# Split halves placed at multiples of 1024 bytes, and held activations stored with high and low half of each element side by side

## The chip, the core and the metric

The kernel runs as one program on one NeuronCore of a Trainium2 chip. Its five engines (TensorE, VectorE, ScalarE, GpSimd and SyncE, in the rows PE, DVE, ACT, POOL and SP) each work through their own list of instructions and meet at semaphores; weights come from HBM through DMA queues into SBUF, the on-chip memory of 128 partitions. PEld in the rows is TensorE's weight load, the reading of the operand that the array holds while the other operand streams through it. The metric is the device time of one execution in microseconds.

## What is computed

Three transformer-like blocks follow each other on one sequence of 256 tokens with 1024 features. Cut to the matrix products that matter here:

```
for layer in range(2):                      # first block
    h = rms_norm(x, g_mix[layer])
    qkv = h @ w_in[layer]                   # 1024 x 3072
    mix = attention of three kinds (differential, block-causal, dilated)
    x = x + mix @ w_out[layer]              # 1024 x 1024
    h2 = rms_norm(x, g_ffn[layer])
    u = causal_conv3(h2 @ w_up[layer])      # 1024 x 5632
    x = x + (silu(gate) * val) @ w_down[layer]   # 2816 x 1024
# second block: a state-space branch and a sparse attention branch, then
h = h + merged @ w_out_2
# expert layer: every token picks 128 of 16384 experts
q = hn @ peer_wq; scores; top-k; gates
act = gelu(hn . u_tab[expert]) * gate       # computed densely: hn @ u_tab.T, 16384 columns
h = h + act @ v_tab                         # 16384 x 1024
return rms_norm(h)
```

Everything is float32, and the result must be close to float32.

## The kernel before

**How a product is made exact.** TensorE reads operands here in the type `float32r`, a shortened float32. To keep the precision, each operand is split into a high half (rounded by the write into an F32R tile) and a low half (the original minus the high half, again rounded). A product is then three matmuls into the same PSUM bank: high with high, high with low, low with high. `mm3` (L536 to L543) writes them out for each step k of the contraction, and nearly all the work of the kernel goes through its line L542. In its calls the first argument pair is held in the array (128 columns), the second is streamed.

**How the weights get in.** The weights are cut into `plan` units of 128 x 1024 floats (512 KB). SyncE loads one unit after the other into the tiles `raw0` to `raw5` (L512), ScalarE writes its high half into `wh` (L1112), and VectorE (L1461) or GpSimd (L2117) writes the low half into `wl`; the list `lower` says which of the two, fixed by the unit's number. Buffers are reused in turn: six of each up to the stage `keys`, four of each in the two last stages.

**Two ways round.** In one kind of stage the weights are held and the activations stream (256 columns for a matmul): the up projection (`wup`, 44 units in each layer), the query projection of the expert layer (`wpq`, 16 units) and the first expert product (`ut`, 128 units). One unit is 8 steps x 3 matmuls = 24 matmuls of 256 columns. In the other kind the activations are held and the weights stream (512 columns): `win` and `wout` (24 and 8 units in each layer), `wdown` (22 in each layer), `wout2` (8) and the second expert product (`vt`, 128). One unit is 12 matmuls of 512 columns. Both ways stream 6144 columns for a unit. A few stages of the second block use whole float32 operands, unsplit (`hw` with `raw`).

**The tiles of activations.** `hh` and `hl` hold high and low half of the normalised and transposed activations, 8 steps of 256 tokens, and serve both kinds of stage; `yh` and `yl` hold those of the gated activations before `wdown`; `ach0/ach1` and `acl0/acl1` those of the expert activations, one unit each. ScalarE writes the high halves (L1142 in `turned`, L1179 in `out_turned`, others inside the stages), VectorE writes the low halves of h (L1511 in `halves_low`) and of the expert activations, GpSimd writes `yl` (L2122). All are written with an element step of one, and the matmuls read them with an element step of one.

**Where the tiles lie.** SBUF is handed out in the order of the `scoped` calls, after 16384 bytes of DMA scratch and a few constants. Start of a tile within 1024 bytes, before and after the change, as the built programs have it:

| tile | before | after |
|---|---|---|
| raw0..3, wh0..3, wl0..3 | 608 | 0 |
| raw4..5, wh4..5, wl4..5 | 0 | 0 |
| hh, hl (after: h2) | 640 | 0 |
| yh, yl (after: y2) | 0 | 0 |
| ach, acl (after: ac0, ac1) | 608 | 0 |

**The order of the work.** It is written out by hand: each engine has one function (`sp`, `pe`, `act`, `dve`, `pool`) that lists its instructions with their waits. Within `ut`, TensorE does `hidden(j)` for unit j, and from `J_GATE` = 59 on also the gate products of four tokens after each unit (`gates_of`). For the units before 59 GpSimd makes the low halves, after that VectorE. In `vt`, each unit waits for its `acl` (L1069) and its low half.

## Time and profile before

| | |
|---|---|
| time, median of 3 runs | 1750.53 us (1750.17 to 1751.01) |
| profiled execution, its span | 1747.2 us |
| PE busy | 1691.7 us (97%), 10714 matmuls |
| PEld busy | 1454.8 us (83%) |
| DVE, ACT, POOL busy | 1149.2, 821.6, 706.5 us |
| HBM read | 279.33 MB, 161 GB/s over the span |

A busy TensorE is not yet a TensorE at its peak: what counts is the **pitch**, the time from the start of one matmul to the start of the next. It can be read from a timeline, or as busy time over count in a stretch without gaps.

### The profile page before, as it was taken

Reading aid. Unit: us, or ns where it says so; the run is one execution under the profiler, and the core shown is the slowest. Engines: PE = TensorE matmul, PEld = TensorE weight load, DVE = VectorE, ACT = ScalarE, POOL = GpSimd, SP = SyncE. Lnnn points to the kernel's source line nnn. Section 1 sums busy time; section 2 is a strip of 40 time slices with the busy share of each in tenths; the row PEclk is TensorE's granted clock in tenths of the full one; section 3 lists DMA queues with packets and bytes.
Section 4 is the critical chain, followed back from the end, with each engine's and each line's share of the span. In section 5 each row is a group of like instructions: output and inputs, shape, how many; then the busy total and the mean of one; then the engine's idle time right before and its main releaser. Section 6 shows DMA issues by size and latency. Waiting matters only on the chain.

```text
span 1747.2 us, 27224 instructions
## 1 busy us (share of the span) xinstructions
PE 1691.7 (97%) x10714; PEld 1454.8 (83%) x10714; DVE 1149.2 (66%) x2422; ACT 821.6 (47%) x1453; POOL 706.5 (40%) x384
## 2 busy tenths in 40 slices
PE   7999999999999998999999999999999999999997
PEld 6779998777799986544579999999999988888885
DVE  6655785756367576666332999999999644444443
ACT  5455665354476642113243554544444455555553
POOL 2424667132357721432163999700000144444443
PEclk9999999999999999999999999999999999999998
DMA  7333545463255564323353656544444566666664
GB/s 292 112 109 132 182 162 195 150 217 108 74 193 190 173 203 134 111 87 109 95 194 134 216 167 198 179 147 145 145 140 139 160 193 193 194 194 195 195 193 134
DMA packets 77455, 283.20 MB, mean 162 GB/s; under 512 B 8720, under 2 KB 8976, under 8 KB 77072
## 3 DMA queue, kind: packets, MB, share of 16 engines
q1 hardware_dynamic: 76032, 276.50, 48.8%
q10 hardware_dynamic: 1296, 4.97, 0.8%
q8 instruction: 85, 1.39, 0.3%
q14 instruction: 42, 0.34, 0.1%
HBM read 279.33 MB, written 2.10 MB: 161 GB/s over the span
## 4 chain that ended last, share of the span: by engine, by line
PE 78%; DVE 8%; ACT 5%; POOL 5%; issue 3%; DMA 1%; POOLq 0%; DVEq 0%; ACTq 0%
PE bank L542 62%; PE bank L533 7%; PE bank L597 5%; POOL wl L2117 4%; ACT wh L1112 2%; DVE att L1478 2%; PE bank L665 1%; DVE wl L1461 1%; ACT att L1115 1%; PE bank L967 1%; PE bank L889 1%; DVE ssb L1467 1%; DVE mix L1506 1%; DVE xs L1467 1%; PE bank L837 0%
## 5 line engine op out<-in xcount | busy, mean ns | idle before, releaser
L2117 POOL TENSOR_TENSOR wl<-raw,wh 128x1024 fp32r<-128x1024 f32 x213 | 548.0, 2584 | 699.6 <-ACT wh L1112 691.1
L542 PE MATMUL bank<-hh,wh 128*128 128x256 f32 x1856 | 526.2, 284 | 5.5 <-POOL wl L2117 4.8
L1112 ACT ACTIVATE wh<-raw 128x1024 fp32r<-128x1024 f32 x476 | 492.7, 1050 | 57.2 <-PE bank L542 40.8
L542 PE MATMUL bank<-hl,wh 128*128 128x256 f32 x1856 | 519.1, 280 | 0.0
L542 PE MATMUL bank<-hh,wl 128*128 128x256 f32 x1856 | 518.1, 279 | 0.0
L1461 DVE TENSOR_TENSOR wl<-raw,wh 128x1024 fp32r<-128x1024 f32 x263 | 352.8, 1347 | 98.7 <-ACT wh L1112 98.2
L542 PEld LDWEIGHTS bank<-hh,wh 128*128 128x128 f32 x1856 | 349.1, 188 | 7.0 <-POOL wl L2117 6.0
L542 PEld LDWEIGHTS bank<-hl,wh 128*128 128x128 f32 x1856 | 349.2, 188 | 0.0
L542 PEld LDWEIGHTS bank<-hh,wl 128*128 128x128 f32 x1856 | 349.0, 188 | 0.0
L1467 DVE TENSOR_TENSOR acl<-H,ach 128x256 fp32r<-128x256 f32 x128 | 87.5, 685 | 181.6 <-ACT ach L1115 181.6
L542 PE MATMUL bank<-wh,ach 128*128 128x512 f32 x512 | 199.3, 389 | 0.4 <-DVE acl L1467 0.4
L542 PE MATMUL bank<-wh,acl 128*128 128x512 f32 x512 | 199.2, 389 | 0.0
L542 PE MATMUL bank<-wl,ach 128*128 128x512 f32 x512 | 199.2, 389 | 0.0
L1115 ACT ACTIVATE H<-bank 128x256 f32<-128x256 f32 (+32 forms) x199 | 64.7, 325 | 240.6 <-PE bank L542 208.0
L1115 ACT ACTIVATE ach<-H 128x256 fp32r<-128x256 f32 x128 | 53.4, 418 | 172.7 <-PE bank L542 172.2
L542 PE MATMUL bank<-wh,hh 128*128 128x512 f32 x288 | 119.3, 414 | 5.5 <-DVE hl L1467 2.9
L1478 DVE SCALAR_TENSOR_TENSOR att<-bank,sml,att 128x255 f32<-128x255 f32 (+1 forms) x176 | 84.4, 480 | 56.7 <-ACT att L1115 53.5
L542 PE MATMUL bank<-wh,hl 128*128 128x512 f32 x288 | 114.1, 396 | 0.0
L542 PE MATMUL bank<-wl,hh 128*128 128x512 f32 x288 | 113.9, 396 | 0.0
L542 PEld LDWEIGHTS bank<-wh,ach 128*128 128x128 f32 x512 | 96.1, 188 | 20.7 <-issue 0.6
L542 PEld LDWEIGHTS bank<-wh,acl 128*128 128x128 f32 x512 | 96.1, 188 | 20.0
L542 PEld LDWEIGHTS bank<-wl,ach 128*128 128x128 f32 x512 | 96.1, 188 | 19.7
(216 smaller groups left out, 2313.4 us busy)
## 6 DMA issues: line engine op xcount, KB each, us to landing
raw<-in_ut_dram SPq DMA_DIRECT2D x128, 512.0 KB, 3.5
raw<-in_vt_dram SPq DMA_DIRECT2D x128, 512.0 KB, 3.8
raw<-in_wup_dram SPq DMA_DIRECT2D x88, 512.0 KB, 4.2
raw<-in_win_dram SPq DMA_DIRECT2D x48, 512.0 KB, 4.6
raw<-in_wdown_dram SPq DMA_DIRECT2D x44, 512.0 KB, 4.2
raw<-in_wout_dram SPq DMA_DIRECT2D x24, 512.0 KB, 3.6
raw<-in_wga_dram SPq DMA_DIRECT2D x16, 512.0 KB, 3.6
raw<-in_wpq_dram SPq DMA_DIRECT2D x16, 512.0 KB, 5.1
```

What stands on the lines that cost most here:

```text
L533: m = p.e.matmul(out, l, r, start=i == 0, stop=i == len(pairs) - 1)
L542: m = p.e.matmul(out, lhs[i][a], rhs[i][b], start=start and i == 0 and j == 0, stop=stop and i == n - 1 and j == 2)
L597: m = p.e.matmul(banks[b][:, 0:cw], whole[:, off + h * kper + k, tcols(t)], unit_whole(i, k, kper, slice(0, cw)), start=h == 0 and k == 0, ...
L665: m = p.e.transpose(banks[b][:, 256 * (i % 2) + 128 * k:256 * (i % 2) + 128 * k + 128], buf[:, o:o + 128], ids[:, :])
L889: s = p.e.matmul(banks[yb][o:o + 32, 0:256], l[:, 32 * n:32 * n + 32], turned_z[n % 2][:, a, b, :], start=j == 0, stop=j == 3, tile_positi ...
L967: m = p.e.matmul(banks[b][:, :], hTw[:, 2 * h + k, tcols(t)], unit_whole(i, k, 2, slice(0, 512)), start=h + k == 0, stop=h + k == 2)
L1112: a.e.activation(high_of(u), raw_of(u), ACTF.Copy).then_inc(act_hi.up(("hi", u)), 1)
L1115: a.e.activation(out, src, f, **kw).then_inc(act_out.up(ev), 1)
L1461: v.e.tensor_tensor(low_of(u), raw_of(u), high_of(u).bitcast(F32), ALU.subtract).then_inc(dve_lo.up(("lo", u)), 1)
L1467: v.e.tensor_tensor(out, a, b, op).then_inc(dve_out.up(ev), 1)
L1478: v.e.scalar_tensor_tensor(out, a, s, b, op0, op1).then_inc(dve_out.up(ev), 1)
L2117: g.e.tensor_tensor(low_of(u), raw_of(u), high_of(u).bitcast(F32), ALU.subtract).then_inc(pool_lo.up(("lo", u)), 1)
```

## The change

Three things are done together:

- Padding is added (a tile `pad0` of 96 floats, `sta` grown to 768, `con` to 1664, `sml` to 896, `R_AT` to 16896), and the DMA scratch is cut from 16384 to 1024 bytes to make room. With it every tile of a split operand starts at a multiple of 1024 bytes (table above).
- `hh`/`hl` become one tile `h2` of 4096 floats with two readings. Before a stage that streams the activations (`halves_for` gives `hT_moving`, norms named "f") it is laid out as before, high half first, then the low half. Before a stage that holds them (`hT_held`) the high half of element i is at 2i and its low half at 2i + 1.
- `yh`/`yl` and `ach`/`acl` become `y2` and `ac2`, always side by side.

So 2928 matmuls (864 with h, 528 with y, 1536 with the expert activations) hold an operand that is read with an element step of 2, and ScalarE, VectorE and GpSimd write, and in part read, these tiles with a step of 2. No instruction is added, removed or moved on any engine, and shapes and types are the same; all that differs besides is that one wait of ScalarE for VectorE inside `ut` falls one weight split later, since `R_AT` has moved.

```
--- before.py
+++ after.py
@@ -100,20 +100,21 @@
...
+        scoped(ctx, "pad0", 96)
         xs = scoped(ctx, "xs", 2048)
...
         sc_h = ExitStack()
-        hh, hl = scoped(sc_h, "hh", 2048, F32R), scoped(sc_h, "hl", 2048, F32R)
+        h2 = scoped(sc_h, "h2", 4096, F32R)
         sc_h.close()
         hw, sel_s = scoped(ctx, "hw", 2048), scoped(ctx, "sel_s", 2048)
-        sta = scoped(ctx, "sta", 760)
+        sta = scoped(ctx, "sta", 768)
         raws = [scoped(ctx, f"raw{i}", 1024) for i in range(4)]
...
         early = ExitStack()
-        con_s = scoped(early, "con", K_W - 128)
-        sml_s = scoped(early, "sml", S_W)
+        con_s = scoped(early, "con", 1664)
+        sml_s = scoped(early, "sml", 896)
         tab_s = scoped(early, "tab", 8192)
...
@@ -127,7 +128,8 @@
...
         sc_f = ExitStack()
-        yTh, yTl = [scoped(sc_f, f"y{c}", NTILE * 256, F32R)[:, :].rearrange("p (k t) -> p k t", k=NTILE) for c in "hl"]
+        y2 = scoped(sc_f, "y2", 2 * NTILE * 256, F32R)[:, :].rearrange("p (k t a) -> p a k t", k=NTILE, a=2)
+        yTh, yTl = y2[:, 0], y2[:, 1]
         sc_f.close()
...
@@ -146,8 +148,8 @@
...
         sc_oh.close()
-        ach = [scoped(ctx, f"ach{j}", 256, F32R)[:, :] for j in range(2)]
-        acl = [scoped(ctx, f"acl{j}", 256, F32R)[:, :] for j in range(2)]
+        ac2 = [scoped(ctx, f"ac{j}", 512, F32R)[:, :].rearrange("p (t a) -> p a t", a=2) for j in range(2)]
+        ach, acl = [a[:, 0] for a in ac2], [a[:, 1] for a in ac2]
         banks = [ctx.enter_context(nc.psum_tensor(f"bank{i}", [128, 512], F32)) for i in range(8)]
...
@@ -282,8 +284,8 @@
...
         x = xs[:, :].rearrange("p (t d) -> p t d", t=2)
-        hTh = hh[:, :].rearrange("p (k t) -> p k t", k=8)
-        hTl = hl[:, :].rearrange("p (k t) -> p k t", k=8)
+        hT_moving = h2[:, :].rearrange("p (a k t) -> p a k t", a=2, k=8)
+        hT_held = h2[:, :].rearrange("p (k t a) -> p a k t", k=8, a=2)
         hTw = hw[:, :].rearrange("p (k t) -> p k t", k=8)
...
@@ -302,8 +304,11 @@
...
-        def hT(k, cols):
-            return hTh[:, k, cols], hTl[:, k, cols]
+        def halves_for(st):
+            return hT_moving if st[0] == "f" else hT_held
+
+        def hT(k, cols, of=hT_held):
+            return of[:, 0, k, cols], of[:, 1, k, cols]
...
@@ -434,8 +439,8 @@
...
         H = H_s[:, :].rearrange("p (j t) -> p j t", j=128)
-        R_AT = 16800
-        assert R_AT >= K_W - 128 + S_W + 8192 + 6144
+        R_AT = 16896
+        assert R_AT >= 1664 + 896 + 8192 + 6144
         r_at = [R_AT]
...
@@ -614,7 +619,7 @@
...
                             m = mm3(banks[b][:, 0:256], [unit_pair(i, k, kt, tcols(c)) for k in range(kt)],
-                                    [hT(off + k, ALLC) for k in range(kt)], True, True, ready)
+                                    [hT(off + k, ALLC, hT_moving) for k in range(kt)], True, True, ready)
                         else:
...
@@ -796,7 +801,7 @@
...
                         m = mm3(banks[b][:, 256 * half:256 * half + 256], [unit_pair(i, k, 8, tcols(0)) for k in range(8)],
-                                [hT(k, ALLC) for k in range(8)], True, True, ready_both(("f", L)))
+                                [hT(k, ALLC, hT_moving) for k in range(8)], True, True, ready_both(("f", L)))
                         m.then_inc(pe_out.up(("used", i), ("up", L, f, half)), 1)
...
@@ -1038,7 +1043,7 @@
...
                 claim(b)
-                m = mm3(banks[b][:, 0:256], [unit_pair(i, k, 8, tcols(0)) for k in range(8)], [hT(k, ALLC) for k in range(8)], True, True, ready_both(("f", 2)))
+                m = mm3(banks[b][:, 0:256], [unit_pair(i, k, 8, tcols(0)) for k in range(8)], [hT(k, ALLC, hT_moving) for k in range(8)], True, True, ready_both(("f", 2)))
                 m.then_inc(pe_out.up(("used", i), ("hid", j)), 1)
...
@@ -1139,7 +1144,7 @@
...
                         a.wait_ge(pe_out, ("T", st, t, k))
-                        do(hTh[:, k:k + n, tcols(t)], quad(ps("T", st, t, k), n), ACTF.Copy, ("hTh", st, t, k))
+                        do(halves_for(st)[:, 0, k:k + n, tcols(t)], quad(ps("T", st, t, k), n), ACTF.Copy, ("hTh", st, t, k))
...
@@ -1161,7 +1166,7 @@
...
             stream_up_to(first["win", 0])
-            load(con_s[:, :], consts_d[:, 128:K_W], con_in, "con")
+            load(con_s[:, 0:K_W - 128], consts_d[:, 128:K_W], con_in, "con")
             load(sml(0, S_W), smalls_d, sml_in, "sml")
...
@@ -1176,7 +1181,7 @@
...
                     a.wait_ge(pe_out, ("mT", L, g))
-                    do(hTh[:, 2 * g:2 * g + 2, :], ps("mT", L, g)[:, :].rearrange("p (k t) -> p k t", k=2), ACTF.Copy, ("mTh", L, g))
+                    do(hT_held[:, 0, 2 * g:2 * g + 2, :], ps("mT", L, g)[:, :].rearrange("p (k t) -> p k t", k=2), ACTF.Copy, ("mTh", L, g))
...
@@ -1506,14 +1511,14 @@
...
-            def halves_low(k0, n, cols, src, hi, ev):
+            def halves_low(of, k0, n, cols, src, hi, ev):
                 v.wait_ge(act_out, hi)
-                tt(hTl[:, k0:k0 + n, cols], src, hTh[:, k0:k0 + n, cols].bitcast(F32), ALU.subtract, ev, alone=True)
+                tt(of[:, 1, k0:k0 + n, cols], src, of[:, 0, k0:k0 + n, cols].bitcast(F32), ALU.subtract, ev, alone=True)
...
                     for k, n in parts(st, q0, nq):
-                        halves_low(k, n, tcols(t), quad(ps("T", st, t, k), n), ("hTh", st, t, k), ("hT", st, t, k))
+                        halves_low(halves_for(st), k, n, tcols(t), quad(ps("T", st, t, k), n), ("hTh", st, t, k), ("hT", st, t, k))
...
@@ -1733,7 +1738,7 @@
...
                 def out_turned(g):
-                    halves_low(2 * g, 2, ALLC, ps("mT", L, g)[:, :].rearrange("p (k t) -> p k t", k=2), ("mTh", L, g), ("mT", L, g))
+                    halves_low(hT_held, 2 * g, 2, ALLC, ps("mT", L, g)[:, :].rearrange("p (k t) -> p k t", k=2), ("mTh", L, g), ("mT", L, g))
...
@@ -2383,7 +2388,7 @@
...
-    nc = _bacc.Bacc("TRN2", target_bir_lowering=False, num_devices=1)
+    nc = _bacc.Bacc("TRN2", target_bir_lowering=False, num_devices=1, dynamic_dma_scratch_size=1024)
     made = layout(inputs)
...
     for name in _ORDER:
```

## Rows read from the trace of the kernel before

**Rows 1.** The page: engines, slices of the span (tenths busy), shares of the chain.
```profile
PE 1691.7 (97%) x10714; PEld 1454.8 (83%) x10714; DVE 1149.2 (66%) x2422; ACT 821.6 (47%) x1453; POOL 706.5 (40%) x384
PEclk9999999999999999999999999999999999999998
PE 78%; DVE 8%; ACT 5%; POOL 5%; issue 3%; DMA 1%; POOLq 0%; DVEq 0%; ACTq 0%
```

**Rows 2.** Chain that ended last, in time: start us, length us, work xcount (512 columns held).
```profile
141.01 5.61 PE bank L542 x24
...
296.02 41.35 PE bank L542 x177
...
611.93 55.18 PE bank L542 x239
...
1386.56 343.02 PE bank L542 x1512
```

**Rows 3.** The same chain, where weights are held (256) or operands are unsplit.
```profile
709.58 6.87 PE bank L597 x16
...
909.01 45.50 PE bank L542 x384
954.51 7.16 PE bank L533 x64
...
1050.23 53.22 PE bank L542 x456
```

**Rows 4.** Timeline of PE, second down projection, round a change of weight buffer: start us, us.
```profile
616.10 0.39 PE L542 MATMUL bank<-wh,yh 128*128 128x512 f32 x1
616.32 0.39 PE L542 MATMUL bank<-wl,yh 128*128 128x512 f32 x1
616.55 0.39 PE L542 MATMUL bank<-wh,yl 128*128 128x512 f32 x1
...
617.46 0.40 PE L542 MATMUL bank<-wh,yh 128*128 128x512 f32 x1
...
619.80 0.39 PE L542 MATMUL bank<-wl,yh 128*128 128x512 f32 x1
```

**Rows 5.** Stretches of the up projections: us, PE (x), PEld, DVE, ACT, POOL, clock, DMA.
```profile
165.00:280.00 115.00, 115.00 (x976) 115.00 (x975) 86.22 (x140) 70.47 (x121) 80.00 (x54) 1.00 0.54 181
505.00:610.00 105.00, 105.00 (x892) 105.00 (x892) 71.95 (x98) 66.44 (x113) 76.91 (x52) 1.00 0.54 181
```

**Rows 6.** Chain in the first expert product, where GpSimd holds it.
```profile
1021.20 19.98 POOL wl L2117 x5
...
1106.51 18.39 POOL wl L2117 x5
```

**Rows 7.** Stretches: attention, `ut` up to unit 59, after it, `vt`; columns as in rows 5.
```profile
20.00:160.00 140.00, 135.89 (x772) 107.94 (x771) 85.02 (x225) 72.39 (x165) 45.31 (x36) 1.00 0.38 125
...
959.00:1128.00 169.00, 164.24 (x1397) 163.02 (x1397) 158.13 (x422) 86.43 (x124) 154.40 (x58) 1.00 0.57 184
1128.00:1386.00 258.00, 258.00 (x2234) 257.93 (x2231) 245.60 (x719) 118.08 (x272) 4.05 (x2) 1.00 0.46 150
...
1400.00:1720.00 320.00, 320.00 (x1413) 265.05 (x1413) 153.45 (x177) 161.45 (x236) 141.16 (x59) 1.00 0.62 193
```

**Rows 8.** Groups: line engine op xcount | busy us, mean ns | idle before, releaser.
```profile
L1467 DVE TENSOR_TENSOR acl<-H,ach 128x256 fp32r<-128x256 f32 x128 | 87.5, 685 | 181.6 <-ACT ach L1115 181.6
...
L1115 ACT ACTIVATE ach<-H 128x256 fp32r<-128x256 f32 x128 | 53.4, 418 | 172.7 <-PE bank L542 172.2 <-DVE H L1467 0.5
L2122 POOL TENSOR_TENSOR yl<-att,yh 128x256 fp32r<-128x256 f32 x44 | 48.6, 1104 | 6.6 <-POOL att L2122 0.5
```

**Rows 9.** Waits of PE: line, waited for, us in total, times, longest.
```profile
PE bank L542 <- POOL wl L2117: 8.5, 11, 1.3
PE bank L542 <- DVE hl L1467: 3.6, 6, 1.1
```

More of the change, by code:

```diff
@@ L101, in scoped @@
             return where.enter_context(nc.sbuf_tensor(name, [128, n], dt))
+        scoped(ctx, "pad0", 96)
         xs = scoped(ctx, "xs", 2048)
@@ L106, in program @@
         sc_h = ExitStack()
-        hh, hl = scoped(sc_h, "hh", 2048, F32R), scoped(sc_h, "hl", 2048, F32R)
+        h2 = scoped(sc_h, "h2", 4096, F32R)
         sc_h.close()
         hw, sel_s = scoped(ctx, "hw", 2048), scoped(ctx, "sel_s", 2048)
-        sta = scoped(ctx, "sta", 760)
+        sta = scoped(ctx, "sta", 768)
         raws = [scoped(ctx, f"raw{i}", 1024) for i in range(4)]
@@ L114, in program @@
         early = ExitStack()
-        con_s = scoped(early, "con", K_W - 128)
-        sml_s = scoped(early, "sml", S_W)
+        con_s = scoped(early, "con", 1664)
+        sml_s = scoped(early, "sml", 896)
         tab_s = scoped(early, "tab", 8192)
@@ L129, in program @@
         sc_f = ExitStack()
-        yTh, yTl = [scoped(sc_f, f"y{c}", NTILE * 256, F32R)[:, :].rearrange("p (k t) -> p k t", k=NTILE) for c in "hl"]
+        y2 = scoped(sc_f, "y2", 2 * NTILE * 256, F32R)[:, :].rearrange("p (k t a) -> p a k t", k=NTILE, a=2)
+        yTh, yTl = y2[:, 0], y2[:, 1]
         sc_f.close()
@@ L148, in program @@
         sc_oh.close()
-        ach = [scoped(ctx, f"ach{j}", 256, F32R)[:, :] for j in range(2)]
-        acl = [scoped(ctx, f"acl{j}", 256, F32R)[:, :] for j in range(2)]
+        ac2 = [scoped(ctx, f"ac{j}", 512, F32R)[:, :].rearrange("p (t a) -> p a t", a=2) for j in range(2)]
+        ach, acl = [a[:, 0] for a in ac2], [a[:, 1] for a in ac2]
         banks = [ctx.enter_context(nc.psum_tensor(f"bank{i}", [128, 512], F32)) for i in range(8)]
@@ L284, in program @@
         x = xs[:, :].rearrange("p (t d) -> p t d", t=2)
-        hTh = hh[:, :].rearrange("p (k t) -> p k t", k=8)
-        hTl = hl[:, :].rearrange("p (k t) -> p k t", k=8)
+        hT_moving = h2[:, :].rearrange("p (a k t) -> p a k t", a=2, k=8)
+        hT_held = h2[:, :].rearrange("p (k t a) -> p a k t", k=8, a=2)
         hTw = hw[:, :].rearrange("p (k t) -> p k t", k=8)
@@ L303, in sml, with halves_for, hT @@
             return sml_s[:, c:c + n]
-        def hT(k, cols):
-            return hTh[:, k, cols], hTl[:, k, cols]
+        def halves_for(st):
+            return hT_moving if st[0] == "f" else hT_held
+        def hT(k, cols, of=hT_held):
+            return of[:, 0, k, cols], of[:, 1, k, cols]
         iota = con(K_IOTA, 128)
@@ L436, in program @@
         H = H_s[:, :].rearrange("p (j t) -> p j t", j=128)
-        R_AT = 16800
-        assert R_AT >= K_W - 128 + S_W + 8192 + 6144
+        R_AT = 16896
+        assert R_AT >= 1664 + 896 + 8192 + 6144
         r_at = [R_AT]
@@ L616, in by_features @@
                             m = mm3(banks[b][:, 0:256], [unit_pair(i, k, kt, tcols(c)) for k in range(kt)],
-                                    [hT(off + k, ALLC) for k in range(kt)], True, True, ready)
+                                    [hT(off + k, ALLC, hT_moving) for k in range(kt)], True, True, ready)
                         else:
@@ L798, in pe @@
                         m = mm3(banks[b][:, 256 * half:256 * half + 256], [unit_pair(i, k, 8, tcols(0)) for k in range(8)],
-                                [hT(k, ALLC) for k in range(8)], True, True, ready_both(("f", L)))
+                                [hT(k, ALLC, hT_moving) for k in range(8)], True, True, ready_both(("f", L)))
                         m.then_inc(pe_out.up(("used", i), ("up", L, f, half)), 1)
@@ L1040, in hidden @@
                 claim(b)
-                m = mm3(banks[b][:, 0:256], [unit_pair(i, k, 8, tcols(0)) for k in range(8)], [hT(k, ALLC) for k in range(8)], True, True, ready_both(("f", 2)))
+                m = mm3(banks[b][:, 0:256], [unit_pair(i, k, 8, tcols(0)) for k in range(8)], [hT(k, ALLC, hT_moving) for k in range(8)], True, True, ready_both(("f", 2)))
                 m.then_inc(pe_out.up(("used", i), ("hid", j)), 1)
@@ L1141, in turned @@
                         a.wait_ge(pe_out, ("T", st, t, k))
-                        do(hTh[:, k:k + n, tcols(t)], quad(ps("T", st, t, k), n), ACTF.Copy, ("hTh", st, t, k))
+                        do(halves_for(st)[:, 0, k:k + n, tcols(t)], quad(ps("T", st, t, k), n), ACTF.Copy, ("hTh", st, t, k))
             def exps(tag, maps, buf, i):
@@ L1163, in act @@
             stream_up_to(first["win", 0])
-            load(con_s[:, :], consts_d[:, 128:K_W], con_in, "con")
+            load(con_s[:, 0:K_W - 128], consts_d[:, 128:K_W], con_in, "con")
             load(sml(0, S_W), smalls_d, sml_in, "sml")
@@ L1507, in scale, with halves_low @@
                                              ).then_inc(dve_out.up(("nrm", st, t, q), ("used", row) if t and q else None), 1)
-            def halves_low(k0, n, cols, src, hi, ev):
+            def halves_low(of, k0, n, cols, src, hi, ev):
                 v.wait_ge(act_out, hi)
-                tt(hTl[:, k0:k0 + n, cols], src, hTh[:, k0:k0 + n, cols].bitcast(F32), ALU.subtract, ev, alone=True)
+                tt(of[:, 1, k0:k0 + n, cols], src, of[:, 0, k0:k0 + n, cols].bitcast(F32), ALU.subtract, ev, alone=True)
             def turned(st, ts_, nq, q0=0):
@@ L2384 @@
     from concourse.bass_utils import run_bass_kernel_spmd as _run
-    nc = _bacc.Bacc("TRN2", target_bir_lowering=False, num_devices=1)
+    nc = _bacc.Bacc("TRN2", target_bir_lowering=False, num_devices=1, dynamic_dma_scratch_size=1024)
     made = layout(inputs)
```

6 lines of the change are left out of this document (3 added, 3 removed).

## The prediction

> **What bounds the kernel now.** I read the page first: PE is busy 97% of the span, at full granted clock in every slice but the last, and 78% of the chain that ended last is PE's [rows 1]. PE waits for other engines only a few microseconds in all [rows 9]. So time can come only out of PE's pitch, the time from one matmul's start to the next, and I read that next, from the chain in order of time.
>
> With held activations and 512 streamed columns the pitch is 343.02/1512 = 226.9 ns in the second expert product, 5.61/24 = 233.8 ns with h, and (41.35 + 55.18)/(177 + 239) = 232.0 ns with y [rows 2]. With held weights and 256 streamed columns it is 53.22/456 = 116.7 ns in the first expert product, 45.50/384 = 118.5 in the query projection [rows 3] and (115 + 105)/(976 + 892) = 117.8 in the up projections [rows 5].
>
> What would it be without any loss? Unsplit float32 passes of 512 columns take 6.87/16 = 429.4 ns, and stream each column at half the pace; half of that, 214.7 ns, is my floor for 512 split columns [rows 3]. Weight loads set a floor of their own: where 128 columns are loaded for short streams the pitch is 7.16/64 = 111.9 ns [rows 3]. So each matmul of 512 loses 12 to 19 ns, and each of 256 some 5 to 7.
>
> **Where the loss depends on addresses.** The telling rows are those of the second `wdown` [rows 4]. Nothing changes there except the weight buffer: the stage begins in the buffers 4 and 5, which start at a multiple of 1024 like y itself, and goes on in 0 to 3, which start 608 bytes off. Before the switch two steps take 616.55 - 616.10 = 0.45 us, 226 ns each or so; after it, from 617.46 to 619.80, ten take 2.34, 234 ns each. The table of tile starts fits it in the other stages: the expert activations start like the weight buffers (both 608) and run at 226.9; h (640) never starts like any weight buffer and runs at 233.8. So equal starts within 1024 bytes are worth 6 to 7 ns of 233. I take the step to be proportional to the columns: a unit has 6144 of them either way, and takes 24 x 116.7 = 2.80 us with 256, and 12 x 233.8 = 2.81 us with 512 at unequal starts.
>
> **The change part by part.** *Alignment, 256 columns.* In all 5568 matmuls the two operands start unlike now (640 against 608 or 0). Half of the aligned 226.9 is 113.4 ns, above the load's floor of 111.9. Gain: 3072 x 3.3 + 384 x 5.1 + 2112 x 4.4 = 10.1 + 2.0 + 9.3 = 21.4 us. Bounds: no gain; a gain down to 111.9, which is 29.7; or, if an aligned matmul loses 12.2 ns however short it is (226.9 - 214.7), 107.4 + 12.2 = 119.6, a loss of about 13. I take the first, since the loss went with the columns above.
>
> *Alignment, 512 columns.* h goes from 233.8 to 226.9 (864 x 6.9 = 6.0 us), y from 232.0 (528 x 5.1 = 2.7), and the expert activations are aligned already. Together 8.7.
>
> *Element step of 2 in what is held.* No row shows a held operand with a step of 2, so it is bounded. The streamed operand moves on by 4 bytes per column. The load takes about twice as long per column (111.9 ns for 128 against 214.7 for 512), so with a step of one it advances at half the stream's pace or less, and the stream overtakes it; with a step of 2 both advance alike, and may get into a fixed relation. The unsplit float32 rows, in which both read at one slow pace, show no loss, but these have slack too. The good end is 214.7 ns. For the bad end: the load touches twice as many bytes' worth of memory, and if the loss comes from that, 12.2 becomes 24.4, 239.1 ns. I take the middle of the good end and the aligned row, (214.7 + 226.9)/2 = 220.8 ns, because equal pace is what differs from the losing rows, and the float32 rows are the nearest ones with equal pace. From 226.9 on that is 2928 x 6.1 = 17.9 us (5.3 with h, 3.2 with y, 9.4 with the experts).
>
> The Trainium skill ("SBUF — State Buffer", specifications) says that an SBUF line is 16 bytes and that two hits in a line suffice for full bandwidth, which a float32 step of 2 just has. No run here shows it; by it the step costs nothing.
>
> *Writes with a step of 2.* ScalarE's write of `ach` (418 ns) and VectorE's of `acl` (685) have 173 and 182 us of idle time ahead of them, over 128 units: even doubled they stay hidden [rows 8]. GpSimd's `yl` (1104 ns, 44 of them) has 80.00 busy of 115 us around it [rows 5]; doubled it would add at most 22 x 1.1 = 24 us to a layer's 35 to 45 of slack. Only h is written on the path, at the start of a stage: PE waits 3.6 us for `hl` [rows 9]. Unchanged it costs 0, doubled 3.6; I take 2.
>
> *What does not get through.* In the attention stages PE is busy 135.89 of 140 us [rows 7], but other engines stand in the chain between its matmuls; of the 11.3 us for h, 768/864 lie there, and I drop 3. Before unit 59, GpSimd holds the chain twice for five low halves (19.98 and 18.39 us, [rows 6]); a faster PE waits longer there, about ten units each at 24 x 3.3 = 79 ns, so I drop 1.6. After unit 59 VectorE is busy 245.60 of 258 us [rows 7]: 12.4 idle for 69 units, or 180 ns each against 79 needed. It covers, thinly; I drop 1. In `vt` ACT, DVE and POOL are busy about half the time and DMA 0.62; a unit at 12 x 220.8 = 2.65 us instead of 2.72 strains none.
>
> **Sum.** 21.4 + 8.7 + 17.9 = 48.0; less 2 + 3 + 1.6 + 1 = 7.6: 40 us. The profiled span of 1747.2 becomes 1707; it lies 3.3 under the median, so the time is 1750.5 - 40 = 1710.5, rounded to 1711.
>
> **The rivals.**
>
> *Alignment only.* The step of 2 does nothing, and 512 columns stay at 226.9 as in the expert stage: 48.0 - 17.9 = 30.1, less some 6.5, is 24: 1727. For it: the aligned expert rows are so steady over 1512 matmuls that they may be the natural pitch.
>
> *Clean.* Equal pace and equal start remove all loss: 214.7 for 512 adds 2928 x 6.1 = 17.9 more, less 2 not passed on: 1695, and 1687 if 256 comes down to 111.9 too. Against it: nothing split runs so today.
>
> *The step of 2 collides (slower).* Its place is PE's weight load beside the stream, in the 128 units of `vt` above all. With 239.1 ns: 1536 x 12.2 = 18.7, 864 x 5.3 = 4.6 and 528 x 7.1 = 3.7, together 27 lost against 21.4 won, plus 2 for the writes: 1758; and 1780 if 256 gains nothing. It decides from a 512 pitch of about 236 (today's mean is 229.9, and 21.4 less 2.6 of deductions over 2928 is 6.4).
>
> *Nothing.* The Trainium skill ("TensorE: Matmul & The Clock Gate", what happens when you issue a matmul) says that TensorE has two independent read ports, and that loading the next weights takes nothing from the running matmul. By that rule, starts and steps of what is held are without effect, and the time stays 1750.5. As a mechanism here: what looks like an effect of the starts [rows 4] would be one of the stage. The trace speaks against it, since pitch switches from 226 to 234 inside one stage.
>
> **How the numbers follow.** Forecast 0.40, alignment only 0.25, clean 0.15, collision 0.13, nothing 0.07. A difference of 0.2% (3.5 us) is what a measurement can tell from no change: faster 0.40 + 0.25 + 0.15 = 0.80, same 0.07, slower 0.13. The range goes from the clean case, where its 256 gains in part (1690), to the no-change case (1752), and leaves out the collision and the extreme of clean, under 0.2.
>
> **What would show it.** In the profile after, per matmul: `vt` at 220.8 instead of 226.9, h and y at the same value as `vt`, `ut` at 113.4, a unit of either kind near 2.65 to 2.72 us, and wup at 113.4 as well. If `vt` stays at 226.9 the step of 2 is idle; at 233 or more it collides. If `ut` stays at 116.7 or moves towards 119.6, the proportion to columns is wrong, and that term of 21.4, the largest, falls. The prediction also fails if the gain appears in PE's pitch but DVE after unit 59 or POOL before it becomes the chain: then PE's idle time there would rise from near zero.

## The result

The changed kernel is slower: 1770.97 us (median of 4 runs, 1770.85 to 1772.19) against 1750.57 us, a ratio of 1.0121 with a 95% interval of 1.0107 to 1.0134, or 20.4 us. The forecast was 1711, with a range of 1690 to 1752; the time lies outside it, and on the other side. The profiled span went from 1747.2 to 1769.2 us.

The page of the changed kernel shows PE busy for the same share of the span as before, at full granted clock: it works longer, and its share of the chain rose from 78% to 87% [rows 1].

```profile
PE 1717.6 (97%) x10714; PEld 1486.3 (84%) x10714; DVE 1144.0 (65%) x2422; ACT 824.0 (47%) x1453; POOL 709.0 (40%) x384
PE 87%; DVE 4%; POOL 4%; ACT 3%; issue 1%; DMA 1%; POOLq 0%; DVEq 0%; ACTq 0%
```

The chain of the changed kernel in order of time (start us, length us, work), the pieces that answer to [rows 2, 3]:

```profile
141.31 5.62 PE bank L547 x24
...
912.78 46.31 PE bank L547 x384
...
1056.14 54.73 PE bank L547 x456
...
1398.65 353.05 PE bank L547 x1512
```

The pitch of the second expert product is now 353.05/1512 = 233.5 ns (226.9 before), that of the first 54.73/456 = 120.0 (116.7), of the query projection 46.31/384 = 120.6 (118.5); with h held it is 5.62/24 = 234.2 (233.8). The up projections, from their stretches (us, PE (x), PEld, DVE, ACT, POOL, clock, DMA), stand at 220/1839 = 119.6 against 117.8 [rows 5]:

```profile
165.00:280.00 115.00, 115.00 (x961) 115.00 (x960) 86.39 (x140) 70.51 (x120) 79.83 (x54) 1.00 0.54 181
505.00:610.00 105.00, 105.00 (x878) 105.00 (x877) 70.47 (x94) 66.94 (x111) 75.86 (x52) 1.00 0.54 178
```

So 1536 x 6.6 = 10.1 us come from the second expert product, 3072 x 3.3 + 384 x 2.1 = 10.9 from the first and its query projection, 2112 x 1.8 = 3.8 from the up projections: 24.8 of pitch. The span grew by 22.0. PE's waits for GpSimd fell from 8.5 to 6.3 us [rows 9], which is most of the difference of 2.8: where another engine held PE before, a slower PE costs nothing.

```profile
PE bank L547 <- POOL wl L2122: 6.3, 9, 1.2
```

The writes with a step of 2 cost next to nothing, as the groups answering to [rows 8] show (busy us, mean ns, idle before): ScalarE's write took 435 ns instead of 418, GpSimd's 1114 instead of 1104.

```profile
L1120 ACT ACTIVATE ac<-H 128x256 fp32r<-128x256 f32 x128 | 55.6, 435 | 182.3 <-PE bank L547 181.9 <-DVE H L1472 0.5
L2127 POOL TENSOR_TENSOR y<-att,y 128x256 fp32r<-128x256 f32 x44 | 49.0, 1114 | 6.6 <-POOL att L2127 0.5
```

### The profile page after: what moved, and what is told of

Read it like the earlier page. It is cut to its first block, busy times and chain, and to the rows that moved or that the text cites. A ratio compares the mean times of both kernels' runs of the same rounds, so it can differ in the third digit from the quotient of the medians.

```text
span 1769.2 us, 27224 instructions
## 1 busy us (share of the span) xinstructions
PE 1717.6 (97%) x10714; PEld 1486.3 (84%) x10714; DVE 1144.0 (65%) x2422; ACT 824.0 (47%) x1453; POOL 709.0 (40%) x384
## 4 chain that ended last, share of the span: by engine, by line
PE 87%; DVE 4%; POOL 4%; ACT 3%; issue 1%; DMA 1%; POOLq 0%; DVEq 0%; ACTq 0%
PE bank L547 70%; PE bank L538 7%; PE bank L602 5%; POOL wl L2122 3%; PE bank L670 1%; ACT wh L1117 1%; PE bank L972 1%; PE bank L894 1%; PE bank L842 1%; DVE mix L1511 1%; DVE xs L1472 1%; POOL ssv L2127 0%; DVE wl L1466 0%; DVE ssb L1472 0%; PE bank L563 0%
## 5 line engine op out<-in xcount | busy, mean ns | idle before, releaser
L547 PE MATMUL bank<-h,wh 128*128 128x256 f32 x3712 | 676.9, 285 | 4.2 <-POOL wl L2122 3.4
L547 PEld LDWEIGHTS bank<-h,wh 128*128 128x128 f32 x3712 | 577.8, 192 | 5.3 <-POOL wl L2122 4.2
L547 PE MATMUL bank<-h,wl 128*128 128x256 f32 x1856 | 525.0, 283 | 0.0
L547 PEld LDWEIGHTS bank<-h,wl 128*128 128x128 f32 x1856 | 355.7, 192 | 0.0
L547 PE MATMUL bank<-wh,ac 128*128 128x512 f32 x1024 | 321.6, 394 | 0.4 <-DVE ac L1472 0.4
L547 PEld LDWEIGHTS bank<-wh,ac 128*128 128x128 f32 x1024 | 197.6, 193 | 42.1 <-issue 0.6
L547 PE MATMUL bank<-wh,h 128*128 128x512 f32 x576 | 196.2, 405 | 6.0 <-DVE h L1472 3.0
L547 PE MATMUL bank<-wl,ac 128*128 128x512 f32 x512 | 201.7, 394 | 0.0
L547 PEld LDWEIGHTS bank<-wh,h 128*128 128x128 f32 x576 | 112.1, 195 | 30.3 <-POOL wl L2122 5.3
L547 PEld LDWEIGHTS bank<-wl,ac 128*128 128x128 f32 x512 | 98.8, 193 | 20.4
L547 PE MATMUL bank<-wl,h 128*128 128x512 f32 x288 | 113.6, 395 | 0.0
```

The costliest lines, as they stand in the source:

```text
L547: m = p.e.matmul(out, lhs[i][a], rhs[i][b], start=start and i == 0 and j == 0, stop=stop and i == n - 1 and j == 2)
```

## The experiments

### The two halves of the change, each alone

`e_align` keeps the starts at multiples of 1024 and stores each half for itself (cut, against the changed kernel):

```
-        y2 = ...rearrange("p (k t a) -> p a k t", k=NTILE, a=2)
+        y2 = ...rearrange("p (a k t) -> p a k t", k=NTILE, a=2)
-        ac2 = [...rearrange("p (t a) -> p a t", a=2) for j in range(2)]
+        ac2 = [...rearrange("p (a t) -> p a t", a=2) for j in range(2)]
-        hT_held = h2[:, :].rearrange("p (k t a) -> p a k t", k=8, a=2)
+        hT_held = hT_moving
```

> The changed kernel with its starts at multiples of 1024, but each half stored for itself (element step 1), so alignment alone. Theory A (step 2 costs the 512-column matmuls some 6.5 ns each, equal starts cost the 256-column ones 2 to 3 ns and win the 512-column ones with h and y): second expert product at 226.9 ns, y at 227 to 228, 256 columns at 120.0; the time lies 10 us (1536 x 6.4 ns) plus some 5 (h and y) under the changed kernel, at 1754 to 1758. Theory B (the step is without effect, and the starts cause all of it): as the changed kernel, 1771, second expert product at 233.3.

`e_step` has the padding, constants and DMA scratch of the kernel before, and the halves side by side (cut, against the changed kernel):

```
-        scoped(ctx, "pad0", 96)
-        sta = scoped(ctx, "sta", 768)
+        sta = scoped(ctx, "sta", 760)
...
-    nc = _bacc.Bacc("TRN2", target_bir_lowering=False, num_devices=1, dynamic_dma_scratch_size=1024)
+    nc = _bacc.Bacc("TRN2", target_bir_lowering=False, num_devices=1)
```

> The kernel before with its padding and its starts (608, 640), but the held activations stored side by side as in the change, so the step of 2 alone. Theory A: second expert product at 233.3 ns instead of 226.9 (+10 us), 256 columns unchanged at 116.7 and 117.8, h and y about as they were: 1760 to 1763. Theory B (the starts cause all of it): 1751, second expert product at 226.9.

Measured: `e_align` 1756.76 us, ratio 1.0038 (1.0023 to 1.0052); `e_step` 1760.77, ratio 1.0060 (1.0043 to 1.0077), both against 1749.97. Their chains, first of `e_align`, then of `e_step`:

```profile
1052.16 54.73 PE bank L547 x456
...
1394.62 343.02 PE bank L547 x1512
```

```profile
1052.59 53.22 PE bank L546 x456
...
1388.97 353.06 PE bank L546 x1512
```

The two losses part cleanly. Alignment alone takes 256 columns to 120.0 ns and leaves the second expert product at 226.9; the step alone takes the latter to 233.5 and leaves 256 columns at 116.7. Theory B of both texts falls. Together they lose 6.8 + 10.8 = 17.6 us of the 20.4. The remaining 2.8 is little more than the spread of the kernel before (1748.87 to 1751.43), but it has the sign of a gain that alignment has only with a step of 1: in `e_align` h is held at 5.48/24 = 228.3 ns, in the changed kernel at 234.2.

```profile
140.67 5.48 PE bank L547 x24
```

### Undoing the loss with 256 columns alone

`e_shift` is the changed kernel with only the streamed reading of h moved on by 32 bytes:

```
-        h2 = scoped(sc_h, "h2", 4096, F32R)
+        h2 = scoped(sc_h, "h2", 4104, F32R)
+        scoped(ctx, "gap", 256)
-        hT_moving = h2[:, :].rearrange("p (a k t) -> p a k t", a=2, k=8)
-        hT_held = h2[:, :].rearrange("p (k t a) -> p a k t", k=8, a=2)
+        hT_moving = h2[:, 8:4104].rearrange("p (a k t) -> p a k t", a=2, k=8)
+        hT_held = h2[:, 0:4096].rearrange("p (k t a) -> p a k t", k=8, a=2)
```

> The changed kernel, step of 2 and all, with only the streamed reading of h moved on by 32 bytes. Theory A: 256 columns fall from 120.0 back to 116.7 in the first expert product and the later up projection, where the held start is equal modulo 256, and by 2 ns in the first; about 3456 x 3.3 = 8 to 11 us and 2112 x 2 to 3 = 4 to 6: 1755 to 1759, with the second expert product still at 233.3. Rival (the loss with 256 columns came from the padding in another way, of ScalarE or GpSimd writes): 1771.

It took 1759.89 us against 1749.09, ratio 1.0062 (1.0046 to 1.0079): 10.8 us over the kernel before, as much as `e_step`, where the changed kernel is 20.4 over. In its chain the first expert product is back at 116.7 and the second still at 233.5. That the loss with 256 columns comes from the streamed start against the held one is thereby shown in the full kernel. The time is just above the 1755 to 1759 that was expected.

```profile
1049.98 53.22 PE bank L548 x456
...
1386.81 353.05 PE bank L548 x1512
```

### A map of starts and steps, without the rest of the kernel

`e_map` is a kernel of its own, all of whose matmuls use one tile B; a section is

```
for i in range(n):
    m0, h0 = mov[i % len(mov)] // 4, HELD + held[i % len(held)] // 4
    lhs = B[:, h0:h0 + 128] if step == 1 else B[:, h0:h0 + 256].rearrange("p (t a) -> p a t", a=2)[:, 0]
    e.matmul(banks[name][:, 0:cols], lhs, B[:, m0:m0 + cols], start=i == 0, stop=...)
```

> A kernel of its own that leaves out all of the computation but matmuls: the array holds 128 columns, 512 or 256 stream, 64 times over the same pair of addresses, in sections that differ in the start of the held operand within 1024 bytes (0 to 896, the streamed one at 0), its element step (1 or 2) and the streamed columns; then the order of tiles of the first and second expert product as before and after. Theory A (two things set the pitch: the relative start and the step): with step 1, 512 columns at offset 0 give about 227 ns and at other offsets about 233; 256 columns give 120 at offset 0 and 117 at some others; with step 2, 512 columns give 233 at offset 0. Theory B (the pitch of the full kernel is not TensorE's own but comes from what the other engines write to SBUF meanwhile): all sections of one length have the same pitch, whatever offset and step, since nothing else runs here, near 215 and 110 ns.

Timeline of PE in `e_map`: start us, length us, and the section's name with streamed columns (m), held step (s) and held start (o); length over count is the pitch plus a few ns, since the length takes in about 0.2 us of tail.

```profile
110.01 14.68 PE L95 MATMUL m512s1o256x<-B 128*128 128x512 f32 x64
...
65.28 15.09 PE L95 MATMUL m512s1o32x<-B 128*128 128x512 f32 x64
...
228.15 15.08 PE L95 MATMUL m512s2o0x<-B 128*128 128x512 f32 x64
...
406.52 7.83 PE L95 MATMUL m256s1o0x<-B 128*128 128x256 f32 x64
...
452.16 7.63 PE L95 MATMUL m256s1o480x<-B 128*128 128x256 f32 x64
...
618.63 9.57 PE L95 MATMUL m320s1o0x<-B 128*128 128x320 f32 x64
...
783.56 8.79 PE L95 MATMUL utnew<-B 128*128 128x256 f32 x72
...
800.73 16.53 PE L95 MATMUL vtold<-B 128*128 128x512 f32 x72
...
833.47 16.96 PE L95 MATMUL vtnew<-B 128*128 128x512 f32 x72
```

Measured from start to start inside each section these are 226.7, 233.4, 233.3, 120.0, 116.7 and 146.7 ns, and 120.0, 226.7 and 233.3 for the orders of tiles of the changed first product and of the second before and after. No other engine runs here, so the pitches are TensorE's own, and theory B falls. The full kernel's values come back, with one miss: the order of the first product before gave 117.8, where the full kernel has 116.7. Held starts of 0, 256, 512 and 768 bytes settle at the same pitch, and so do 128, 384, 640 and 896: in the starts tried the pattern repeats every 256 bytes, not every 1024.

From 256 to 512 columns at equal starts the pitch grows by 106.7 ns, 0.417 ns a column, which is columns/2.4. Over that, equal starts with step 1 lose 13.3 ns at 256, 320, 384 and 512 columns, 15.8 at 448, and 10.0 to 12.0 at 264, 272 and 288 (the last three from `e_map_fine`). The loss is not the same at every length, but it is no share of the columns.

### Is the load's reading the cause?

`e_map_fine` varies the start in finer steps, and the held columns. In its names b is how many bytes the streamed operand starts after the held one.

> Again a kernel that leaves out all of the computation but matmuls over one pair of addresses in each section. The streamed operand starts 4 to 224 bytes after the held one within 256 bytes (so the held one lies that much before it), held step 1; then fewer held columns (32, 64, 96), steps of 3 and 4, and 240 to 288 streamed columns. Theory C (the loss is the weight load's reading: one 2.4 GHz cycle for each 16-byte line of the held operand, 32 lines with step 1, which gives 512 columns + 32 cycles = 226.7 ns and 256 + 32 = 120.0): with 64 held columns 16 lines, so 220.0 and 113.3 ns; with 32 columns 216.7 and 110; step 4 touches 128 lines and costs most, above 240 ns. Theory D (the loss belongs to the start of each streamed operand, whatever is loaded beside it): no dependence on the count of held columns, 226.7 and 120.0 with 32 and with 96 alike, and none on the step. For the offsets both expect a dependence of some ns with period 256; the question is whether a start gives 256 columns less than 116.7 ns.

```profile
66.65 7.42 PE L81 MATMUL m256b16x<-B 128*128 128x256 f32 x64
73.90 7.98 PE L81 MATMUL m256b20x<-B 128*128 128x256 f32 x64
...
477.72 7.42 PE L81 MATMUL m256h64x<-B 128*64 128x256 f32 x64
...
503.50 15.10 PE L81 MATMUL m256s4x<-B 128*128 128x256 f32 x64
...
548.27 14.89 PE L81 MATMUL m512h64x<-B 128*64 128x512 f32 x64
```

Neither theory holds as put. 64 held columns give 113.3 ns with 256 (as C has it, against D), but 229.9 with 512, more than the 226.7 of 128 held columns (against C's 220.0). A loss of one cycle for each line read by the load is not the rule. What stands is that the pitch depends on where load and stream read relative to each other, and changes within 4 bytes of start: with 256 columns 16 bytes gave 113.3 and 20 gave 122.3. The loss over columns/2.4 ran from 6.7 ns (16 bytes) to 16.6 (4 bytes) with 256 columns and from 13.4 to 23.3 with 512, where 0 and 28 bytes were the best (226.7) and 4 the worst (236.6).

`e_steps` varies the element step of either operand, with equal starts.

> Matmuls alone: steps 1 to 4 of the held operand under 64 to 512 streamed columns, then steps 2 and 4 of the streamed one, all starts equal. Theory F (a step of 2 makes the load itself slower, and the pitch with 256 columns is the load's): with 64 and 128 streamed columns step 2 is slower than step 1's 111.6 ns, at 120 or more; steps 3 and 4 give 173 and 233 whatever is streamed, up to 256 columns. Theory G (the load is as fast with step 2, 111.6 ns, and what costs is its meeting with a full stream): step 2 equals step 1 under 64 and 128 columns and differs only under 512. A streamed step of 4 touches a new 16-byte line with each column and should cost most of all: 512 columns well over 300 ns.

```profile
186.67 8.71 PE L75 MATMUL m192held2x<-B 128*128 128x192 f32 x72
195.22 12.75 PE L75 MATMUL m192held3x<-B 128*128 128x192 f32 x72
...
234.07 8.80 PE L75 MATMUL m256held2x<-B 128*128 128x256 f32 x72
255.18 16.96 PE L75 MATMUL m256held4x<-B 128*128 128x256 f32 x72
...
343.00 16.96 PE L75 MATMUL m512held2x<-B 128*128 128x512 f32 x72
359.80 17.11 PE L75 MATMUL m512held3x<-B 128*128 128x512 f32 x72
...
502.91 32.69 PE L75 MATMUL m512streamed2x<-B 128*128 128x512 f32 x72
```

Where the load is what limits (192 streamed columns), step 1 gave 111.7 ns in the first map, step 2 gives 118.8, step 3 174.8; with 256 columns steps 2, 3 and 4 give 120.0, 173.3 and 233.3. So the load does get slower with the step, a little at 2 and in proportion from there on (59.4, 58.3 and 58.3 ns for each element of step), as theory F has it. At equal starts step 2 costs nothing with 256 columns (120.0 at either step) or with 384 (173.3 at either), but 6.6 ns with 512 (233.3 against 226.7), where the load has over 100 ns to spare. F does not explain that; what is left is a meeting with the stream (G), whose working is not shown. Step 3 adds hardly more (235.6). No start that was tried brought a step of 2 with 512 columns and 128 held ones under 230.0 ns (192 bytes).

A streamed step of 2 doubles the pitch (451.2 ns with 512 columns): the stream takes its columns at half the pace. Step 4 does cost most, as expected (461.3), but hardly more than step 2, which was not.

The control with 64 and 128 columns failed: those sections opened the kernel and ran at 213.3 ns at steps 1 to 3, where the first map had 111.6 with 128. The trace shows why. Its records of the granted clock start only 181.7 us into this run, and there, in the middle of one section, the pitch falls from 213 to 111.6 ns; the views print 1.00 for the time before, for which there is no record. Later the clock is recorded at half its full level for 13.7 us, and the first matmuls of 256 columns, at the end of that stretch, are again 213 ns apart; the next are 120 apart:

```profile
175.72 4.53 PE L75 MATMUL m192held1x<-B 128*128 128x192 f32 x20
213.00:224.00 11.00, 11.00 (x48) 11.00 (x48) 0.00 (x0) 0.00 (x0) 0.50 0.00 0
224.84 1.48 PE L75 MATMUL m256held1x<-B 128*128 128x256 f32 x6
```

So the opening sections most likely ran at the lower of TensorE's two clock levels (1.2 GHz), and say nothing on theories F and G. The rows used above lie in stretches recorded at full clock.

### Several rhythms for the same addresses

For one relative start, the held operand 64 bytes after the streamed one (or, modulo 256, the streamed one 192 after the held), the first map had given 117.8 ns and the fine one 113.3. `e_orders` put the promising starts into the kernel's orders of tiles; `e_entered` entered the same pairs after one matmul of 128 to 352 columns.

> Again matmuls alone, now in the order of tiles of the first expert product (eight steps, high and low halves, 256 columns) and of the second (512 columns), at the starts that stood out in the two maps. Theory A (the start of the streamed operand relative to the held one, modulo 256 bytes, sets the pitch, whichever tiles take turns): 16 bytes later gives 113.3 ns in the first order, 32 gives 116.7, 0 gives 120.0, at every base; in the second order 0 and 28 give 226.7, all others and step 2 give 230 to 237. Rival (the pitch depends on absolute starts or on how a section began, since 64 bytes gave 117.8 in one map and 113.3 in the other): the same relative start gives different pitches at different bases, and 113.3 is lost when tiles take turns.

> Matmuls alone once more. The same pairs (256 columns, streamed operand 0, 16, 32 or 192 bytes later) and the same orders (first expert product at 192; second at 0 with step 1 and with step 2) are entered after one matmul of another length (128 to 352 columns). Theory E (several steady rhythms belong to the same addresses, and which one is taken depends on how the run began): some pairs, the one at 16 above all, show different pitches in different sections (113.3, 116.6, 118.7), while those of the changed kernel (0 with 256 columns: 120.0; 0 with step 2 and 512: 233.3) stay the same however entered. Theory A without it (addresses alone decide): each pair has one pitch whatever it is entered from, and the base of both operands is without effect.

Two rows of `e_orders`, the order of the first product with 16 bytes at two bases, then rows of `e_entered`, where "lead" is the length of the matmul ahead:

```profile
138.18 8.71 PE L96 MATMUL ut16base64x<-B 128*128 128x256 f32 x72
146.73 8.56 PE L96 MATMUL ut16base128x<-B 128*128 128x256 f32 x72
```

```profile
88.37 8.80 PE L100 MATMUL m256b0lead352x<-B 128*128 128x256 f32 x72
...
105.61 8.61 PE L100 MATMUL m256b16lead160x<-B 128*128 128x256 f32 x72
...
122.67 8.34 PE L100 MATMUL m256b16lead224x<-B 128*128 128x256 f32 x72
130.98 8.71 PE L100 MATMUL m256b16lead288x<-B 128*128 128x256 f32 x72
...
274.28 17.16 PE L100 MATMUL vt0s2lead160x<-B 128*128 128x512 f32 x72
...
299.67 16.51 PE L100 MATMUL vt0lead224x<-B 128*128 128x512 f32 x72
```

In `e_orders` 16 bytes gave 116.7 or 118.7 ns depending on the base, never theory A's 113.3; 112 and 192 bytes gave 113.3. In `e_entered` one and the same pair, 16 bytes apart, settles at 116.7, 113.3 or 118.7 ns within its first matmuls and keeps that value for the whole section. The length of the one matmul before is what differs, and it matters by itself: leads of 192 and 224 columns both came after a section of this pair at 116.7, and gave 116.7 and 113.3. Theory E is shown for this pair (and for 192 bytes: 113.3 or 117.8), and the plain form of theory A (addresses alone decide) falls. For what concerns the change it does no harm: 0 bytes with 256 columns settles at 120.0 however it is entered, 32 bytes at 116.7, 512 columns with step 1 at 226.7, and with step 2 at 233.3 or 235.6, never less.

### Versions that beat both kernels

All have step 1, all tiles at multiples of 1024, and the streamed reading of h moved on by 32 (`e_best`), 16, 192 or 112 bytes; against `e_align`:

```
-        h2 = scoped(sc_h, "h2", 4096, F32R)
+        h2 = scoped(sc_h, "h2", 4104, F32R)
+        scoped(ctx, "gap", 256)
-        hT_moving = h2[:, :].rearrange("p (a k t) -> p a k t", a=2, k=8)
-        hT_held = hT_moving
+        hT_moving = h2[:, 8:4104].rearrange("p (a k t) -> p a k t", a=2, k=8)
+        hT_held = h2[:, 0:4096].rearrange("p (a k t) -> p a k t", a=2, k=8)
```

> Step 1 everywhere, all tiles at multiples of 1024, and the reading of h for the stages that stream it 32 bytes further on (a gap of 1024 bytes makes room), so each kind of stage has the relative start that was best in the map: held and streamed equal for 512 columns, streamed 32 bytes later for 256. Theory A: 256 columns at 116.7 ns in all stages (from 120.0), 512 at 226.7 in all; against the kernel before y gains 528 x 5 = 2.7 us, the up projections 2112 x 1.1 = 2.3, h up to 864 x 6 = 5: 1740 to 1745 us. Rival (the relative start acts only in the stages where it was changed by chance, and h gains nothing because other engines stand between its matmuls): 1745 to 1750.

> As the version with streamed h 32 bytes later, but 16 bytes later. Theory A: 256 columns at 113.3 ns, a unit of the first expert product 2.72 instead of 2.80 us; the up projections give 2112 x 3.4 = 7.2 us, the query projection 1.3, the first expert product 3072 x 3.4 = 10.4 less what POOL before unit 59 and DVE after it hold back (some 3): 15 to 18 us under that version's 1745, so 1727 to 1731. Rival: the pitch gained is held back by POOL and DVE in the whole first expert product, whose time stays; then only the up projections gain, 1737. Second rival: in the running kernel 113.3 does not hold, 1745.

> Streamed h 192 bytes later than the held starts, the place that gave 113.3 ns in the orders. Theory A: 256 columns at 113.3 in the full kernel; up projections minus 7 us, query projection and first expert product minus 11.7, less what POOL and DVE hold back: 1727 to 1732. Theory E: the rhythm is lost when each unit's first matmul waits or other matmuls stand between; then the up projections may run at 113.3 and the first expert product at 117 to 118: 1738 to 1748.

> As before it, with 112 bytes. Theory A: the same 1727 to 1732. Theory E: 1738 to 1748. If one of the two is fast and the other is not, the rhythm depends on more than the relative start.

| bytes | time us | before, same chip | ratio | 95% interval |
|---|---|---|---|---|
| 32 | 1745.13 | 1750.76 | 0.9969 | 0.9957 to 0.9981 |
| 16 | 1744.73 | 1749.04 | 0.9976 | 0.9967 to 0.9985 |
| 192 | 1742.34 | 1749.23 | 0.9960 | 0.9946 to 0.9974 |
| 112 | 1744.15 | 1749.23 | 0.9967 | 0.9956 to 0.9978 |

All are faster than both kernels by a little. 32 bytes came out at the edge of theory A's 1740 to 1745, 16 bytes at its second rival's 1745, 192 and 112 in theory E's 1738 to 1748; theory A's 1727 to 1732 never came. Two things stand against it. The first is the rhythm, in the chain of `e_best192`:

```profile
964.90 57.41 PE bank L548 x504
...
1133.00 2.83 PE bank L548 x24
1136.72 2.74 PE bank L548 x24
```

The first units of the first expert product do run at 57.41/504 = 113.9 ns, later ones before unit 59 at 117.8. From unit 59 on, the gate products stand between the units, each unit is entered anew, and a unit takes 2.83 or 2.74 us in turn: the rhythm of 113.3 is caught only every other time.

The second is that other engines take the gain back. The last version, 112 bytes, ran at about 113.5 ns in both up projections and at 113.3 in nearly all units before 59, and is still no faster than the one with 32 bytes at 116.7 (0.9967 against 0.9969). From the first to the sixtieth unit's start, the first expert product took 172.4 us in the kernel before, 172.0 in `e_best` and 174.4 in `e_best112`: there VectorE's work on the tile `H` became the chain, and PE waited for it (3.8 us at once, after which the granted clock was at half for 3.4 us; that costs an estimated 1.5 us, and without it the time would still be no shorter than in `e_best`). The first up projection took 124.6 us at 118.0 ns (before), 124.6 at 116.7 (`e_best`) and 124.4 at 113.6 (`e_best112`). A stretch of it, first of `e_best`, then of `e_best112` (us, PE (x), PEld, DVE, ACT, POOL, clock, DMA), has PE idle more and no more matmuls done:

```profile
165.00:275.00 110.00, 109.09 (x933) 108.81 (x932) 84.41 (x136) 66.50 (x114) 75.56 (x51) 1.00 0.54 178
165.00:275.00 110.00, 107.04 (x931) 105.99 (x930) 84.53 (x136) 66.35 (x113) 75.65 (x51) 1.00 0.54 181
```

The second up projection did get shorter, from 123.2 to 120.6 us, and `wdown` after it longer by 2.7. PE's waits, first in `e_best192`, then in `e_best112`, are

```profile
PE bank L548 <- POOL wl L2123: 12.5, 15, 1.4
```

```profile
PE bank L548 <- POOL wl L2123: 15.0, 16, 1.5
PE bank L1056 <- DVE H L1473: 3.8, 1, 3.8
```

against 8.5 for GpSimd and none for H before [rows 9].

## Why the prediction was wrong

**What bounds the kernel** was right for a slower PE: the loss of 20.4 us is pitch, less what PE's waits gave back. For a faster PE it was right only in part (see the covers). That the starts of held and streamed operand against each other matter was right too, and was read off correctly from the switch inside `wdown` [rows 4]; the map repeats both values (226.7 and 233.4).

**Alignment with 256 columns** is the first step that failed: "I take the step to be proportional to the columns". It rested on one coincidence, that a unit takes 2.80 us with 24 matmuls of 256 and 2.81 with 12 of 512 at unequal starts. But the two kinds had different relative starts, and the 256-column stages already had one of the better ones (streamed 32 bytes later, 116.7 ns, with the buffers 0 to 3). At equal starts a matmul loses 13.3 ns over its bare columns with 256 as with 512. The bound that the prediction itself named for this, 119.6 ns and a loss of about 13 us, was nearly exact (120.0, and 3072 x 3.3 + 384 x 2.1 + 2112 x 1.8 = 14.7 us). The term was given as a gain of 21.4: an error of 36 us.

**The step of 2** is the second: 220.8 ns was taken, as the middle of the good end and the aligned row, because equal pace was hoped to help. Measured were 233.3 to 234.2 with all three operands. The unsplit float32 rows were the wrong neighbour: there the stream runs at half pace, and no run tells whether a disturbance would show. The term was given as a gain of 17.9 and is a loss: 2928 x (233.3 - 226.7) = 19.3 us against aligned step 1, 37 us of error. The rival "collides" had its place and half its price (239.1 instead of 226.9 was forecast, 233.3 measured), at a chance of 0.13. It combined its loss with a gain or with no change at 256 columns, 1758 or 1780, and so bracketed the result by luck, without having its parts.

**Alignment with 512 columns**: right in `e_align` (h 228.3, y near 227), where it was forecast as 8.7 us; in the changed kernel the step takes all of it back. The three terms with their measured sizes, 8.7 - 14.7 - 19.3, make a loss of 25.3 us of pitch, and the stages showed 24.8.

**The covers** were right for the writes with a step of 2, which stayed hidden, and in that waits absorb part of a pitch, here in the changed kernel's favour (24.8 of pitch, 22.0 of span). For a faster PE they were far too small, a third step that failed, though it did not decide this result. The prediction took 2.6 us off for the first expert product and nothing for the up projections. But in the first up projection and before unit 59 the better pitch of `e_best112` gave nothing (124.4 us for 124.6, 174.4 for 172.0), and even with its 113.4 ns the term of 21.4 would not have come through: `e_best112` has that pitch in most of its 256-column matmuls and 226.7 in the second product, the "alignment only" rival's terms, and gained 5 to 6 us (0.9967), where that rival had 24. The reading behind it, that PE waits "only a few microseconds in all", went by two rows of the view [rows 9]. All its rows together come to 43 us, and 22% of the chain was not PE's from the start [rows 1]; the longest row is

```profile
PE bank L558 <- DVE mix L1506: 9.4, 4, 8.7
```

Whether VectorE after unit 59 would hold a steady 113.3 was not tested, since no version ran so fast there.

**The Trainium skill.** "TensorE: Matmul & The Clock Gate" (what happens when you issue a matmul) says that loading the next weights does not steal bandwidth from the running matmul. The map disagrees for float32r: with nothing else running, moving the held operand by 32 bytes takes 512 columns from 226.7 to 233.4 ns. "SBUF — State Buffer" (specifications) wants two hits in each 16-byte line for full bandwidth; that agrees roughly with the load, which hardly slows at a step of 2 (111.7 to 118.8 ns) and then takes 174.8 and 233.3 at 3 and 4. For a streamed operand it does not agree: a step of 2 doubles the pitch. By that page the held step would have cost nothing, and with 256 and 384 columns at equal starts it does; with 512 it costs 6.6 ns.

**The chances.** 0.80 for faster was far too sure. Both unknown terms had a bound on the other side, and the forecast took the good part of each; with both bad bounds the prediction's own sum (13 lost at 256 columns, 27 in the collision, 2 for the writes) would have been a loss of some 40.

**What stays open** is the mechanism of the disturbance. That the pitch depends on the load's addresses and step against the stream's, with a period of 256 bytes in the starts tried and with several stable rhythms, is shown; where the two meet and why is not, and the simple count of lines fell.

## What to carry to other kernels

Where weights are loaded beside a full-rate stream, place held and streamed tiles on purpose and measure the pitch of each length apart: what is best for 512 columns (equal starts) was one of the poorer places for 256 (120.0, against 116.7 with 32 bytes between). A loss that is equal in two kinds of work may be equal by chance; before it is called proportional, ask what else differs between them. A small kernel that runs matmuls alone over one tile gave the big kernel's pitches after the change (120.0 and 233.3) and one of its two before (226.7, but 117.8 for 116.7), so such a question can be put in one run before any layout is changed. But a pitch won there may not last between other matmuls, and other engines may take it back: ask in which stages a faster TensorE would find its operands ready.

## What the runs showed of the hardware that was not expected

- The same pair of addresses has up to three steady pitches (113.3, 116.7, 118.7 ns with 256 columns and 16 bytes between), chosen by the length of one matmul before it.
- The load takes 111.7, 118.8, 174.8 ns per 128 columns at element steps 1, 2, 3 (with 192 columns streamed) and 233.3 at 4 (256 streamed). With 512 streamed columns, steps 2, 3 and 4 cost alike: 233.3, 235.6 and 235.1 against 226.7; with 256 and 384 step 2 costs nothing at equal starts.
- A streamed step of 2 takes 512 columns from 226.7 to 451.2 ns; a step of 4 gives 461.3.
- A load with a step of 4 keeps its pace when TensorE's granted clock halves: with 128 columns streamed, both steps 4, `e_steps` had 233 ns a matmul from 419.2 to 420.7 us, at full clock, and 233 after that, in a stretch recorded at half. The pitch of 256 columns with step 1 went from 120 to 213.
